# Conditioning sums of the first part: from TensorE to VectorE, and fourteen small loads from the Scalar queue to the GpSimd queue

## The reference, cut to what matters

```python
c_act = jax.nn.silu(c)                                    # c: (1, 1024)
mod = (c_act @ ada_w[l] + ada_b[l])[:, None, :]           # ada_w: (1024, 6144)
sh1, sc1, g1, sh2, sc2, g2 = jnp.split(mod, N_MOD, axis=-1)
h = rms_norm(x, pre_norm_mix[l]) * (1.0 + sc1) + sh1      # x: (1, 1024, 1024)
y = hybrid_mixer(h, ...)                                  # begins with u = h @ w_in
```

## Time and profile before

| what | us |
|---|---|
| median of three runs | 1055.84 |
| the profiled execution, its own time | 1059.57 |
| its span in the profile | 1057.6 |
| TensorE busy | 956.4 (90%) |
| VectorE busy | 518.7 (49%) |
| ScalarE busy | 303.8 (29%) |
| GpSimd busy | 204.3 (19%) |
| first projection matmul starts at | 38.20 |

### The profile page before, as it was taken

One profiled execution on the slowest core, in us unless ns is written; L12 is line 12 of the kernel. 1 busy time (PEld: TensorE's weight loads), 2 busy tenths in 40 slices (PEclk: granted clock), 3 DMA queues, 4 the chain that ended last, 5 costly groups with the idle time before them and its releaser, 6 DMA issues. The chain is left out here.

```text
span 1057.6 us, 12534 instructions
## 1 busy us (share of the span) xinstructions
PE 956.4 (90%) x4356; PEld 498.6 (47%) x4356; DVE 518.7 (49%) x956; ACT 303.8 (29%) x587; POOL 204.3 (19%) x247
## 2 busy tenths in 40 slices
PE   5899999999999999996999999747999998999946
PEld 2344444444456566666666665433333333333312
DVE  2454337444845555556477875563333332333326
ACT  3310001222534334331232232103333333333313
POOL 2200000222600500002244312012222221222003
PEclk9999999999989999998999999957999999999968
DMA  8983442000000000004011121994999999997547
GB/s 316 379 320 147 160 159 50 0 1 0 7 0 1 1 1 2 1 1 199 1 72 69 60 81 70 399 393 168 352 423 393 421 403 408 408 411 310 203 203 285
DMA packets 48981, 192.38 MB, mean 182 GB/s; under 512 B 15586, under 2 KB 20754, under 8 KB 32402
## 3 DMA queue, kind: packets, MB, share of 16 engines
q1 hardware_dynamic: 40196, 173.10, 41.9%
q0 software_dynamic: 7056, 18.36, 4.6%
q10 hardware_dynamic: 1664, 0.07, 0.1%
HBM read 174.21 MB, written 24.64 MB: 188 GB/s over the span
## 5 line engine op out<-in xcount | busy, mean ns | idle before, releaser
L1555 PE MATMUL PS<-ring,xg_T 128*64 x368 | 166.3, 606 | 3.0 <-ACT near_gu L1732 2.0
L1555 PE MATMUL PS<-near_gu,xg_T 128*64 128x512 f32 x368 | 166.3, 606 | 0.0
L1454 PE MATMUL PS<-w_out_sb,cat_T 128*128 128x512 f32 x256 | 118.0, 602 | 4.1 <-DVE y_sc L1875 2.8
L980 PE MATMUL PS<-hT,w_in_sb 128*128 128x512 f32 x256 | 112.2, 599 | 1.2 <-DVE hT L703 1.2
L1555 PEld LDWEIGHTS PS<-ring,xg_T 128*64 128x64 f32 x368 | 51.3, 140 | 110.1 <-issue 110.1
L414 POOL TENSOR_SCALAR rstd<-stat 128x1 f32<-128x1 f32 (+1 forms) x48 | 22.4, 467 | 394.9 <-ACT junk L582 198.8
L1581 PE MATMUL PS<-ring,hid_T 128*64 x184 | 83.8, 598 | 0.4 <-DVE hid_T L2090 0.4
L1581 PE MATMUL PS<-near_dn,hid_T 128*64 128x512 f32 x184 | 83.9, 598 | 0.0
L2081 DVE TENSOR_TENSOR hid<-PS,hid_s 128x128 f32<-128x128 f32 x46 | 11.2, 286 | 147.0 <-ACT hid_s L1714 147.0
L879 DVE TENSOR_REDUCE row_max<-PS 128x1 f32<-128x1024 f32 (+7 forms) x64 | 48.2, 753 | 65.6 <-PE PS L1126 65.5
L1124 PE MATMUL PS<-kT,qT 96*128 96x512 f32 (+4 forms) x192 | 78.5, 520 | 0.0
(11 more groups left out here) (329 smaller groups left out, 1520.4 us busy)
## 6 DMA issues: line engine op xcount, KB each, us to landing
ring<-in_w_gate_dram SPq DMA_DIRECT2D x32, 1024.0 KB, 8.8
ring<-in_w_up_dram SPq DMA_DIRECT2D x32, 1024.0 KB, 11.3
ring<-in_w_down_dram SPq DMA_DIRECT2D x32, 1024.0 KB, 14.6
ada_later<-in_ada_w_dram SPq DMA_DIRECT2D x16, 1024.0 KB, 4.8
ada_first<-in_ada_w_dram SPq DMA_DIRECT2D x8, 1024.0 KB, 8.5
y_g<-y_rows SPq DMA_DIRECT2D x8, 1024.0 KB, 11.9
x_in<-in_x_dram SPq DMA_DIRECT2D x8, 512.0 KB, 8.7
w_in_sb<-in_w_in_dram SPq DMA_DIRECT2D x4, 1024.0 KB, 13.1
```

Source lines behind the costliest of these rows:

```text
L980: last = pe.matmul(BANK[4 + n % 4][:, :], w_in_sb[:, k, XC0 + ct * P:XC0 + (ct + 1) * P], hT[:, k, hh * HALF:(hh + 1) * HALF], start=(k == ...
L1454: last = pe.matmul(BANK[6 + j], cat_T[t % 2][:, k, :], w_out_sb[:, k, j * HALF:(j + 1) * HALF], start=(k == 0), stop=(k == KC - 1))
L1555: last = pe.matmul(BANK[2 + b][rows_, :], xg_T[b][:, k, rows_], gu[u][:, :, k, :], start=(k == 0), stop=(k == KC - 1))
```

## The change

Three things move. (1) The eight chunks of the first part are summed by VectorE with `ada_chunk`, between its other work on the first tiles, instead of by TensorE with `first_mod`. (2) The sum over partitions becomes 16 matmuls: for each of the 16 output columns q, a strided slice of `acc` (128 x 128) is the stationary operand and one column of ones the moving one. The copy to `mod_rows4` and the four transposes are gone. (3) The fourteen small loads are issued by POOL, behind its inverse roots of the first four tiles, instead of by ACT at its start. `acc_ready` counts one less.

```diff
@@ SP
-                        sp.wait_ge(S["acc_ready"], 2)
+                        sp.wait_ge(S["acc_ready"], 1)
@@ POOL
             for t in range(FIRST):
                 inverse_root(pool, 0, t, S["sq_done"], t + 1)
+            pool.dma_start(pre1_col[:, :], col(pre_norm_mix)).then_inc(S["small_loaded"], 16)
...
+            pool.dma_start(rb_row[:, NG:], rows(b_expert_router[0].rearrange("g e -> (g e)"))).then_inc(S["small_loaded"], 16)
             for t in range(FIRST, NT):
                 inverse_root(pool, 0, t, S["sq_done"], t + 1)
@@ ACT
-            act.dma_start(pre1_col[:, :], col(pre_norm_mix)).then_inc(S["small_loaded"], 16)
...
-            act.dma_start(rb_row[:, NG:], rows(b_expert_router[0].rearrange("g e -> (g e)"))).then_inc(S["small_loaded"], 16)
             act.wait_ge(S["c_loaded"], 16)
             act.activation(c_act[:, :], c_col[:, :], ACT.Silu).then_inc(S["c_ready"], 1)
@@ DVE
+            dve.wait_ge(S["c_ready"], 1)
+            ada_chunk(0)
             normed(0)
             normed(1)
+            ada_chunk(1)
             raw_half(0)
             raw_half(1)
             normed(2)
             normed(3)
+            ada_chunk(2)
             raw_half(2)
             raw_half(3)
+            ada_chunk(3)
+            ada_chunk(4)
             dve.wait_ge(S["small_loaded"], 16 * SMALL)
             dve.tensor_copy(pos_f[:, :], pos_i[:, :]).then_inc(S["consts_T"], 1)
-            dve.wait_ge(S["ada_step"], KC)
-            dve.tensor_copy(mod_rows4[:, :], BANK[4]).then_inc(S["acc_ready"], 1)
+            for n in range(5, KC):
+                ada_chunk(n)
 
             dve.wait_ge(S["mod_summed"], 1)
-            link(dve.tensor_tensor(modc[:, :].rearrange("p (r k) -> p r k", k=KC // 2),
-                                   BANK[5].rearrange("p (k r j) -> p r k j", k=KC // 2, r=4)[:, :, :, 0],
-                                   b1_col[:, :, :].rearrange("p s (g k) -> p (s g) k", g=2), ALU.add))
+            link(dve.tensor_tensor(modc[:, :], BANK[4][:, 0:2 * KC], b1_col[:, :, :].rearrange("p s k -> p (s k)"), ALU.add))
@@ PE
-            x_T(0)
-            x_T(1)
-            first_mod(0)
-            x_T(2)
-            first_mod(1)
-            x_T(3)
-            for k in range(2, KC):
-                first_mod(k)
+            for t in range(FIRST):
+                x_T(t)
             pe.wait_ge(S["consts_T"], 1)
             n = (TAPS + 1) * NCT
             pe.transpose(BANK[7][:, 0:n], conv_rows[:, :], ident[0:n, 0:n])
             pe.transpose(BANK[7][:, P:P + NT], pos_f[:, :], ident[0:NT, 0:NT]).then_inc(S["consts_T"], 1)
-            pe.wait_ge(S["acc_ready"], 1)
-            for k in range(KC // 2):
-                last = pe.transpose(BANK[5][:, k * P:(k + 1) * P], mod_rows4[:, k * P:(k + 1) * P], ident[:, :])
+            pe.wait_ge(S["ada_step"], KC)
+            for q in range(2 * KC):
+                a0 = q // KC * D + q % KC
+                last = pe.matmul(BANK[4][:, q:q + 1], acc[:, a0:a0 + D - KC + 1:KC], ones[:, 0:1],
+                                 start=True, stop=True)
             last.then_inc(S["mod_summed"], 1)
```

More of the change, by code:

```diff
@@ L155, in hybrid_block @@
         acc = place("acc", R_S, [P, 2 * D])
-        mod_rows4 = place("mod_rows4", R_S, [P, HALF])
         ada_first = [place(f"ada_first{i}", R_X + 8192 * i, [P, 2 * D]) for i in range(4)]
@@ L448, in _ @@
                 inverse_root(pool, 0, t, S["sq_done"], t + 1)
+            pool.dma_start(pre1_col[:, :], col(pre_norm_mix)).then_inc(S["small_loaded"], 16)
+            half = P // 2
+            pool.dma_start(cat_gain[0:half, :], ssd_norm[0].rearrange("(p k) -> p k", k=KC)).then_inc(S["small_loaded"], 16)
+            pool.dma_start(cat_gain[half:P, :], mla_out_norm[0].rearrange("(p k) -> p k", k=KC)).then_inc(S["small_loaded"], 16)
+            pool.dma_start(conv_rows[0:TAPS * NCT, :], conv_w[0].rearrange("j (n p) -> (j n) p", p=P)).then_inc(S["small_loaded"], 16)
+            pool.dma_start(conv_rows[TAPS * NCT:, :], conv_b[0].rearrange("(n p) -> n p", p=P)).then_inc(S["small_loaded"], 16)
+            pool.dma_start(pos_i[:, :], positions[0].rearrange("(n p) -> n p", p=P)).then_inc(S["small_loaded"], 16)
+            pool.dma_start(dtb[:, :], rows(dt_bias[0])).then_inc(S["small_loaded"], 16)
+            pool.dma_start(a_row[:, :], rows(a_log[0])).then_inc(S["small_loaded"], 16)
+            pool.dma_start(dsk[:, :], rows(d_skip[0])).then_inc(S["small_loaded"], 16)
+            pool.dma_start(qn_col[:, :], col(q_norm)).then_inc(S["small_loaded"], 16)
+            pool.dma_start(kvn_col[:, :], col(kv_norm)).then_inc(S["small_loaded"], 16)
+            pool.dma_start(b1_col[:, :, :], ada_b[0, 0:ROW0].rearrange("(s p k) -> p s k", s=2, k=KC)).then_inc(S["small_loaded"], 16)
+            pool.dma_start(rb_row[:, 0:NG], rows(b_group_router[0])).then_inc(S["small_loaded"], 16)
+            pool.dma_start(rb_row[:, NG:], rows(b_expert_router[0].rearrange("g e -> (g e)"))).then_inc(S["small_loaded"], 16)
             for t in range(FIRST, NT):
@@ L777, in _ @@
             dve.wait_ge(S["small_loaded"], 16 * SMALL)
-            dve.wait_ge(S["acc_ready"], PARTS)
+            dve.wait_ge(S["acc_ready"], PARTS - 1)
             assert NCT == NT
@@ L919, in x_T @@
                 last.then_inc(S["xT_done"], 1)
-            def first_mod(k):
-                if k == 0:
-                    pe.wait_ge(S["c_ready"], 1)
-                buf, i, loads = ada_place(k)
-                pe.wait_ge(S[f"ada_loaded{i}"], 16 * loads)
-                for r in range(4):
-                    cols = buf[:, r // 2 * D:(r // 2 + 1) * D].rearrange("c (p k) -> c k p", k=KC)[:, r % 2 * (KC // 2):(r % 2 + 1) * (KC // 2), :]
-                    last = pe.matmul(BANK[4][32 * r:32 * (r + 1), :], c_act[:, k:k + 1].to_broadcast([P, 32]), cols,
-                                     start=(k == 0), stop=(k == KC - 1))
-                last.then_inc(S["ada_step"], 1)
-            x_T(0)
-            x_T(1)
-            first_mod(0)
-            x_T(2)
-            first_mod(1)
-            x_T(3)
-            for k in range(2, KC):
-                first_mod(k)
+            for t in range(FIRST):
+                x_T(t)
             pe.wait_ge(S["consts_T"], 1)
```

2 lines of the change are left out of this document (1 added, 1 removed).

## The result

Beside each other on one chip, the kernel before took 1055.82 us (median of 4) and the changed one 1066.84 us (median of 4, from 1063.25 to 1067.32). The ratio over all their executions is 1.0097 [1.0078, 1.0116], a loss of 10.2 us (8.2 to 12.2); the two medians are 11.0 apart. The prediction was 1064.5 us within 1059.0 to 1071.5. The profiled execution took 1066.13 us, its span is 1064.4 us.

The account below looks back on a forecast made before the run. TensorE, busy for 90% of the span, was taken as the bound. Accumulation +1.3, partition sums +4.9, small loads +1.6, clock +0.8 and hand-over rounding 0.1 made +8.7 on the median 1055.84: 1064.5 us, range 1059.0 to 1071.5.

Parts of the forecast that it names:

- The carry: From TensorE's first projection unit to the end: a shift of that unit's start reaches the end one to one.
- Step 1: VectorE's chain from chunk 0 at 13.05: 23.69 us of work, accumulation ends at 36.8 instead of 35.51, +1.3 us.
- Step 2: Sum over partitions on TensorE: 32 records at 0.20, 6.4 us (3.9 to 7.0) in place of 1.47, +4.9 us.
- Step 3: Small loads issued by POOL: VectorE's conversion waits for the last from 29.4 to 31.0, +1.6 us (0 to 7.6).
- Step 4: First unit on TensorE: the engine arrives at the lower clock and stays there longer, +0.8 us (0 to 1.8).
- Small loads gate: Rival at VectorE's conversion: POOL's issues are held up, wait 7.1 instead of 1.6, shift 14.2, 1070.0 us; chance 18%.
- The clock turns: Rival on TensorE: full clock within the sums, which cost 3.9, unit 6.9, 1059.4 us; 19% with small terms falling low.

Follow-up runs that it names:

- second pair: The kernel before and the changed kernel, each run and profiled once more unchanged: 1051.82 us (one execution) and 1065.23 us.
- sums_only: The changed kernel with the small loads back on ACT's queue: 1066.07 us, ratio 1.0097 to the kernel before.
- warm_sums: The changed kernel with unread filler matmuls on TensorE while VectorE accumulates, ahead of the partition sums: 1064.35 us, ratio 1.0099 to the kernel before.
- plain_weights: The changed kernel with 128 neighbouring columns of acc as weights instead of every eighth, summing the wrong features: 1063.19 us, one execution.
- conversion_last: The changed kernel with the positions' conversion behind the last chunk and its two transposes behind the sums: 1064.30 us, ratio 1.0084 to the kernel before.
- strip_sums: The changed kernel with four strip matmuls (ones as weights, acc moving), a copy and four transposes for the partition sums: 1060.11 us, ratio 1.0042 to the kernel before.
- strip_fill: The kernel strip_sums with filler matmuls on TensorE, three behind the transposes of x and five between chunks: 1061.12 us, ratio 1.0056 to the kernel before.
- small_on_sp: The kernel before with the small loads issued by SP between the loads of chunks 3 and 4: 1056.48 us, ratio 1.0023 to the kernel before.

## Why the prediction was right, point by point

**The carry.** TensorE's work is the bound from the first unit on, and a shift there reaches the end. The table shows it for ten kernels, within its intervals. The traces show it more closely up to the last matmul with `w_in_sb`; before, then after (ns min/median/max, first and last start):

```profile
L1012 PE MATMUL PS<-w_in_sb,hT x128: 519/519/519, 165.1 to 264.0; 128*128 128x424 f32 x128
```

```profile
L999 PE MATMUL PS<-w_in_sb,hT x128: 519/519/519, 173.6 to 272.6; 128*128 128x424 f32 x128
```

The first unit ended 8.55 later and the last of these starts 8.6 later; in the second pair it is 9.66 and 9.6 (262.6 and 272.2). Behind it the profiles differ by more than their conditioning explains. From this start to the end of the span it takes 787.2 to 793.7 us in the five profiles with TensorE's old conditioning work, and 788.6 to 794.2 in the nine others. That is why the spans of the first pair are only 6.8 apart and those of the second 13.4, and why the loss is read from the ratios of many executions.

**Step 1, +1.3 forecast for the chain itself.** The time between chunk 0 and the end of the chunks, without the conversion's wait, was to be 36.8 - 13.05 = 23.75; measured 36.58 - 11.59 - 1.57 = 23.4. The start was off: chunk 0 landed 1.46 earlier. The prediction had this as its lower bound, from the small packets that go one for one with the large, and sums_only, with these packets back, has 13.40. Taken with the wait below, the accumulation ended 1.07 later than before, and not 2.9. So the shift of 1.46 was won by moving the small loads, and the wait that they brought took 1.57 back.

**Step 2, +4.9 forecast, +6.35 measured.** This is the term that was mis-sized. The prediction took 0.20 us a record from the 36-column matmuls at 307.41 us; measured 0.243, so that it takes 7.82 from accumulation to the end of the sums against 1.47. That was above its bound of 7.0. The reason given for it was also wrong: it put the 0.20 down to the lower clock and kept 0.12 as the price at the full clock. By warm_sums the price does not hang on the clock: ten records in two microseconds at either level. That it is the weight load is inferred from the one column that each record moves and the 0.335 us that the load shows. The 0.12 of the earlier trace rows belongs to one-column transposes, which show as one record each, with a load of 0.200 us, and were no measure for this kind; plain_weights gives 0.025 of the 0.243 to the stride.

The Trainium skill, "TensorE: Matmul & The Clock Gate", section "LDWEIGHTS (loading the stationary operand)", would have 0.107 us for such a load, and this trace has 0.335 for a float32 one. As an estimate by that rule the sums were to take 3.4 us. The measurement decides. The 0.214 between starts in plain_weights is twice the 0.107.

**Step 3, +1.6 forecast, 1.57 measured (2.00 in the second profile).** The issues ended at 20.2, near the lower end of 19.3 to 24.7, and the last landing took 9.6, near the upper end of its rows. The agreement is partly luck: VectorE was to reach the conversion at 29.4 and the last load to be there at 31.0, and it was 27.75 and 29.3, both some 1.7 earlier. The prediction also counted each microsecond of the wait as one at the end, and did not see what stands behind it: without it (conversion_last) 0.86 of 2.00 come back, since the chunks' loads are late next.

**Step 4, +0.8 forecast.** Against the first profile of before the unit is 9.87 - 8.74 = 1.1 longer. But the four other profiles with that work have 7.11, and against these the five profiles of the one-column form with all terms in place (8.81, 9.29, 9.47, 9.87, 10.06) lose 1.7 to 3.0. The step that failed here is its baseline: it took one execution's 8.74 for what the kernel before always pays. In all five TensorE had stood for 6.5 us or more before the sums, the granted clock was 0.50 in the sums, and it was still 0.50 when the unit began. The prediction's reason, that the engine arrives at the lower level, does not explain this by itself. In strip_sums TensorE stood for 6.51 us too and the strips ran at 0.50, yet the clock was 1.00 when the unit began, and it took 7.11. In warm_sums TensorE did not stand and the sums began at 1.00, yet the clock fell within them and the unit took 10.16. All seven profiles with one-column sums have a unit of 8.63 to 10.16; strip_fill, with 8.80, shows that it can be long without them. For the first profile of the changed kernel:

```profile
50.50:51.00 0.50, 0.50 (x2) 0.13 (x1) 0.28 (x1) 0.41 (x3) 0.42 (x2) 0.50 1.05 393
...
51.50:52.00 0.50, 0.50 (x3) 0.26 (x2) 0.00 (x0) 0.41 (x2) 0.42 (x2) 1.00 1.05 393
```

The clock comes back between 51 and 51.5, 5.4 to 5.9 us into the unit.

**The sum.** Forecast 8.7 us; in the first pair of profiles the unit's end moved by 7.42 + 1.13 = 8.55, in the second by 9.66, and the ratio gives 10.2 (8.2 to 12.2). In the first pair the terms are 1.07, 6.35 and 1.13: step 2 came 1.45 dearer, steps 1 and 3 together 1.83 cheaper. The closeness of the sum owes something to these two misses that cancel.

**The rivals.** "Small loads gate" did not come: the fourteen issues took 9.04 us in all, 0.65 each, those beside the two-input chunks at 0.51 to 0.59, and the conversion waited 1.57. "The clock turns" did not come and could not have saved the 2.5 us that it counted for the sums, by warm_sums.

What stays open: why the same kernel's granted clock in the first unit was 0.50 in one profile and 1.00 in another. The profiled spans of before, 1057.6 and 1049.8 us, show that such differences go on later:

```profile
core 0: 1057.6 us, clock 0.957
```

```profile
core 0: 1049.8 us, clock 0.966
```

## What to carry to other kernels

Idle time on an engine is not a gain by itself: moving the accumulation into it ended it 1.07 us later, because the loads set the pace anyway, and most of the loss came from the sum over partitions that it made necessary, at a point where TensorE's stream can't start without it. When a sum over partitions stands on the path, make the long operand the moving one and the ones the weights (3.85 us with its copy and transposes), and not the reverse (7.8 us). A shift ahead of a bound engine's stream is worth what its first unit's end says, start and length together, and the length should be read from more than one profile.

## What the runs showed of the hardware

- A float32 matmul of one column with new weights of 128 columns costs 0.243 us a record and shows as two (after), 0.218 with neighbouring columns as weights (plain_weights). Ten such records fill two microseconds at a granted clock of 1.00 and at 0.50 (warm_sums). Eight records of 512 columns with 32 output rows took 2.02 us at 1.00 (strip_fill) and 2.04 at 0.50 (strip_sums).
- The granted clock fell in the middle of one-column matmuls that left no gap in PE or PEld (warm_sums).
- The same fourteen small loads, 0.07 MB, were 1664 packets on ACT's queue and 448 on POOL's. In 18 to 22 us a packet was recorded with 0.01 us on ACT's queue (before) and 0.146 on POOL's (after), where POOL's earlier ones had 0.014.
- An issue of a DMA by POOL took 0.64 to 1.11 us beside one-input operations of VectorE on 128 rows and 0.51 to 0.59 beside two-input ones (after).
- Small packets ahead of a large load in one queue cut the traffic of 18 to 22 us to 0.14 MB (small_on_sp), where with small packets in another queue 1.31 MB passed (before).
